# Rotary rounding one tile step later, and VectorE's query units behind the next maximum, in a hybrid decoder layer

## The reference, cut to what matters

```python
q = (_rmsnorm(c_q, q_norm_g) @ w_uq).reshape(b, s, MLA_HEADS, QK_NOPE + QK_ROPE)      # 8 heads, 64 + 32
kv = (_rmsnorm(c_kv, kv_norm_g) @ w_ukv).reshape(b, s, MLA_HEADS, QK_NOPE + V_HEAD)
q_rope = _apply_rope(q_rope, cos[:, :, None, :], sin[:, :, None, :])   # x1*cos - x2*sin, x2*cos + x1*sin
k_rope = _apply_rope(k_rope_raw, cos, sin)
...
sc = jnp.einsum('bqhd,bkhd->bhqk', qn, k_nope) + jnp.einsum('bqhr,bkr->bhqk', qr, k_rope)
sc = jnp.where(causal[None, None], sc.astype(jnp.float32) * scale, -jnp.inf)
p = jax.nn.softmax(sc, axis=-1).astype(v.dtype)
return jnp.einsum('bhqk,bkhd->bqhd', p, v)
```

## Time and profile before

| | |
|---|---|
| median of 3 runs | 2233.1 us (2231.65 to 2235.87) |
| the profiled execution | 2231.14 us, span 2229.3 us, mean granted TensorE clock 0.992 |
| PE busy over the span | 2145.4 us (96%) |
| DVE, ACT, POOL busy | 1367.7 us (61%), 979.3 us (44%), 405.3 us (18%) |
| attention's tile steps | about 1237 to 1441 us from the span's start |

### The profile page before, as it was taken

How to read it: one execution, slowest core, us unless ns; L and a number is a source line. 1 busy time by engine, 2 the same in 40 slices (tenths; PEclk the granted TensorE clock), 3 DMA queues, 4 the chain that set the end, 5 groups by cost and what they waited for, 6 DMA issues and landing times.

```text
span 2229.3 us, 25934 instructions
## 1 busy us (share of the span) xinstructions
PE 2145.4 (96%) x9837; PEld 1780.6 (80%) x9837; DVE 1367.7 (61%) x1719; ACT 979.3 (44%) x1559; POOL 405.3 (18%) x444
## 2 busy tenths in 40 slices
PE   5999999999999999999999888899899999999998
PEld 4888788878887888888888677788788888888886
DVE  7667865557587656211212788677856766557666
ACT  6443333334364776311323666545533333333444
POOL 3123320000032221000011455402213331000012
PEclk9999999999999999999999999999999999999999
DMA  3355442253442111222410100265335453216234
GB/s 123 95 171 186 159 166 71 68 196 102 153 161 84 52 52 50 76 67 66 134 43 25 29 10 10 104 218 194 108 103 190 165 193 119 71 51 228 94 137 156
DMA packets 220293, 249.85 MB, mean 112 GB/s; under 512 B 24261, under 2 KB 161546, under 8 KB 220170
## 3 DMA queue, kind: packets, MB, share of 16 engines
q1 hardware_dynamic: 220170, 248.19, 34.0%
HBM read 192.06 MB, written 55.57 MB: 111 GB/s over the span
## 4 chain that ended last, share of the span: by engine, by line
PE 86%; DVE 6%; ACT 3%; issue 2%; POOL 2%; DMA 0%; SPq 0%; POOLq 0%; ACTq 0%; DVEq 0%
PE ps L88 28%; PE ps L90 28%; PE ps L89 28%; PE ps L2322 1%; PE ps L2290 1%; ACT a_probs L2266 1%; POOL a_rot L2207 1%; DVE a_pt L98 1%; PE ps L361 0%; DVE a_s L2256 0%; DVE w_lo L98 0%; DVE entry_y L346 0%; DVE exit_x L1337 0%; DMA entry_x<-in_x_dram 0%; DVE ff_w_lo L98 0%
## 5 line engine op out<-in xcount | busy, mean ns | idle before, releaser
L98 DVE TENSOR_TENSOR ff_w_lo<-ff_raw,ff_w_hi 128x512 fp32r<-128x512 f32 x264 | 214.0, 814 | 171.8 <-ACT ff_w_hi L94 171.5
L88 PE MATMUL ps<-ff_t,ff_w_hi 128*128 128x512 f32 x704 | 274.1, 389 | 0.4 <-DVE ff_w_lo L98 0.2
L90 PE MATMUL ps<-ff_t,ff_w_lo 128*128 128x512 f32 x704 | 273.9, 389 | 0.0
L89 PE MATMUL ps<-ff_t,ff_w_hi 128*128 128x512 f32 x704 | 273.9, 389 | 0.0
L94 ACT ACTIVATE ff_w_hi<-ff_raw 128x512 fp32r<-128x512 f32 x264 | 164.9, 627 | 179.5 <-PE ps L90 173.0
L88 PE MATMUL ps<-d_b_hi,d_a_hi 128*128 128x512 f32 x608 | 237.5, 391 | 3.8 <-DVE d_a_lo L98 3.7
L90 PE MATMUL ps<-d_b_hi,d_a_lo 128*128 128x512 f32 x608 | 236.6, 389 | 0.0
L89 PE MATMUL ps<-d_b_lo,d_a_hi 128*128 128x512 f32 x608 | 236.6, 389 | 0.0
L98 DVE TENSOR_TENSOR w_lo<-w_raw,w_hi 128x1024 fp32r<-128x1024 f32 (+2 forms) x81 | 90.5, 1119 | 233.2 <-ACT w_hi L94 233.2
L88 PE MATMUL ps<-ff_b,ff_w_hi 128*128 128x512 f32 x528 | 208.0, 394 | 6.0 <-ACT ff_u2x L696 5.0
L89 PE MATMUL ps<-ff_b,ff_w_hi 128*128 128x512 f32 x528 | 206.8, 392 | 0.0
(11 more groups left out here) (301 smaller groups left out, 4297.6 us busy)
## 6 DMA issues: line engine op xcount, KB each, us to landing
ff_raw<-in_ffn_w_gate_dram SPq DMA_DIRECT2D x44, 512.0 KB, 3.9
ff_raw<-in_ffn_w_up_dram SPq DMA_DIRECT2D x44, 512.0 KB, 4.0
d_sums<-in_ffn_w_down_dram SPq DMA_DIRECT2D x44, 512.0 KB, 4.1
sums_scratch<-d_sums SPq DMA_DIRECT2D x88, 256.0 KB, 2.6
w_raw<-in_w_in_dram SPq DMA_DIRECT2D x32, 512.0 KB, 4.0
d_raw<-sums_scratch SPq DMA_DIRECT2D x24, 512.0 KB, 3.3
w_raw<-in_w_out_dram SPq DMA_DIRECT2D x24, 512.0 KB, 4.2
spill_scratch<-ff_st SPq DMA_DIRECT2D x44, 256.0 KB, 2.9
```

The source lines that it names most:

```text
L88: pe.matmul(out, lh, rh, start=start, stop=False, skip_group_check=go_on)
L89: pe.matmul(out, lh, rl, start=False, stop=False, skip_group_check=go_on)
L90: return pe.matmul(out, ll, rh, start=False, stop=stop, skip_group_check=go_on)
L98: return nc.vector.tensor_tensor(lo, src, as_f32(hi), ALU.subtract)
```

## The change: what it does

In `act_step` and `dve_step` the rope's rounding and low part are those of unit n - 2 and no longer n - 1. In `dve_step` a q unit is worked on one tile step later (step n + 1, behind the maximum of n + 1, the low parts of n - 1, rope's low part of another unit and `pair_lo`); a k unit stays in step n. In `pool_step` the normalisation of n comes ahead of the rope sum of n - 1. TensorE's order and ScalarE's unit rounding stay. No instruction is added or taken away.

```diff
         if n < HEADS * HEAD_TILES:
-            if n > 0 and self.beside(n - 1):
-                self.rope_act(act, self.beside(n - 1))
+            if n > 1 and self.beside(n - 2):
+                self.rope_act(act, self.beside(n - 2))
             self.exponent(act, n)
             if self.beside(n):
                 self.unit_act(act, self.beside(n))
@@ dve_step
         if n >= 2:
             self.turned_lo(dve, n - 2)
         if n < HEADS * HEAD_TILES:
-            if n > 0 and self.beside(n - 1):
-                self.rope_dve(dve, self.beside(n - 1))
+            if n > 1 and self.beside(n - 2):
+                self.rope_dve(dve, self.beside(n - 2))
             if s == 3 and h > 0 and h % 2 == 0:
                 self.pair_lo(dve, h // 2 - 1, slice(0, SEQ), h // 2)
             if n == HEADS * HEAD_TILES - 1:
                 self.pair_lo(dve, 3, half_of(0), 4)
-            if self.beside(n):
+            before = self.beside(n - 1) if n > 0 else None
+            if before and before[0] == "q":
+                self.unit_dve(dve, before)
+            if self.beside(n) and self.beside(n)[0] == "k":
                 self.unit_dve(dve, self.beside(n))
 
     def pool_step(self, pool, n):
+        self.normalise(pool, n)
         if n > 0 and self.beside(n - 1):
-            pool.wait_ge(self.S["norm_done"], 2 * n)
+            pool.wait_ge(self.S["norm_done"], 2 * n + 2)
             self.rope_pool(pool, self.beside(n - 1))
-        self.normalise(pool, n)
```

## The result

The changed kernel takes 2245.86 us (median of 4 runs, 2245.62 to 2248.57) against 2232.38 before: 13.5 us slower, ratio 1.0061 with an interval of 1.0044 to 1.0079. The forecast was 2239.9, slower, and its range ended at 2245.0. The profiled execution spans 2244.0 us, 14.7 more than before. All of it lies in the tile steps: from the first scores of head 0 to the last product it is 224.3 us (1232.35 to 1456.66) for 209.6 (1232.99 to 1442.55), 14.75 more. The changed kernel's trace comes to these first scores 0.64 us earlier, in work that the change doesn't touch, so that its last product starts only 14.1 us later.

A forecast was written before the change was run, and what follows sets the result against it. TensorE bounds the kernel (busy 176 of 204 us in the tile steps), VectorE nearly as full (162). Terms 5.2 + 2.0 - 0.4 = +6.8 us on the profiled 2231.1 give 2237.9, plus 2.0 to the median: 2239.9; 8-in-10 range 2232.5 to 2245.

The forecast's parts named there:

- Place 1: Hand-over from step 7 to the next head's step 1, 7 times: TensorE's wait moves from `turn` to the unit; +5.2 us.
- head 6: Hand-over from head 6 to 7, without a unit at step 1: low parts of tile 7 about 0.3 us later.
- Place 2: Step 3 of odd heads, 3 times: maximum of step 6 0.96 us late, 0.68 us carried into the hand-over; +2.0 us.
- rival (b): VectorE's lateness from step 3 is taken up before step 7, hand-overs cost nearer 0.5 each: +2.6 us, 2235.7; chance 0.25.
- Place 3: Step 1 of even heads, 4 times: earlier low parts against a later exponent and maximum, clock included; -0.4 us.
- The waits for exponents: TensorE's waits for exponents in the tile steps, 4.8 us before the change, would nearly go.
- The clock term of 0.7 us: Even heads of the kernel before: 0.7 us taken as lost to the lower clock behind the wait before `turn` of tile 2.
- Head 0: Scores of step 4 no longer wait 1.50 us for an exponent behind rope: 0.6 us gained.
- GpSimd's order: Rope sum behind the normalisation at the hand-over: costs nothing, since the sum already followed the normalisation of tile 7.
- rival (c): Longer TensorE pauses end at the lower clock; four more falls of 0.7 us add 2.8: 2242.7; chance 0.12.
- the upper end of (c): By the skill's rule each of nine new TensorE pauses is a candidate for a clock fall: 2246.

The follow-up runs named there:

- only7: The kernel before with the change made for the q units of step 7 alone: 2242.78 us, ratio 1.0044.
- ropes: The changed kernel with VectorE's q unit back in its own step, rope later and GpSimd's sum behind the normalisation: 2246.91 us, ratio 1.0065.
- ropes_pf: The kernel before with only rope's rounding and low part a step later, GpSimd's sum still ahead of the normalisation: 2234.68 us, ratio 1.0008.
- full_pf: The changed kernel with GpSimd's rope sum ahead of the normalisation again: 2255.88 us, ratio 1.0106.
- filled kernels: The changed kernel and the kernel before, each with unread transposes in nearly all TensorE pauses of the tile steps: 2240.91 and 2229.42 us.
- after_fill2: The changed kernel with unread transposes in nearly every TensorE pause of the tile steps: 2240.91 us, ratio 1.0040.
- only3: The kernel before with the change made for the q units of step 3 of odd heads alone: 2238.30 us, ratio 1.0027.

## Why the prediction was wrong, point by point

- **Place 1** was right, mechanism and size. At full clock the hand-over costs +0.60 to +0.63 us from even and about +0.94 from odd heads (only7), forecast 0.7 and 0.93; head 6 +0.26, forecast 0.3. The gain at `turn` (1.80 to 0.75) and its loss at the unit came as the sum had them.
- **Place 2** had the mechanism (VectorE idles for 1.93 us, the wait goes from tile 3 to tile 4), but the term was over-sized: 2.0 us forecast, OA +0.13 and about 0.10 us beyond place 1 in OB, 0.7 us for three heads. The maximum of step 6 does come late, 0.98 us by its distance from the product of step 3 (13.51 for 12.53, forecast 0.96), but OA is only 0.13 longer: most of it is taken up by step 7, which was rival (b).
- **Place 3** was under-sized: -0.4 us forecast. At full clock EA is +1.0 to +1.1 us in heads 2, 4 and 6, where my steps amount to 0.4 to 0.6 without the clock's share. The prediction has the path: rope's rounding and low part ahead of the maximum of step 4. What it didn't have is the weights' low part, lengthened by 0.74 us beside GpSimd's sum: ScalarE's `take` ends at 1295.35, but `add` starts at 1295.98, when that low part has ended, so `add`, `pair_hi` behind it and rope's rounding behind that are late by up to 0.6 us. By this timeline `turn` of tile 2 comes 0.30 us earlier than before and not 0.98, and some 0.5 of the 1.08 us are the lengthened low part, an estimate; no run took it out alone. The waits for exponents didn't go either (4.5 us), since a new one of 0.76 us stands in each even head. The clock term of 0.7 us for the kernel before was right: filling gives back 0.67 us each in heads 2 and 6. Head 0 gained 0.3 us ahead of its first product, forecast 0.6.
- **GpSimd's order** "costs nothing": wrong as a statement. It is worth 12 us with VectorE's unit early (ropes against ropes_pf) and the opposite, 10 us, with it late (full_pf). Within this change it was the better of the two, and the places where it helps or hurts were not in the sum.
- **The step that failed is the clock.** Without it, my terms for the order from head 0's first product to head 6's hand-over, 5.2 + 2.0 + 1.6 us, come to 8.8, and the filled kernels show 8.8 over the same heads. That this agrees is luck: place 1 measured 4.9, place 2 0.7 and place 3 3.1. For the clock, the sum took 1.4 us as given back in heads 2 and 6 and set down nothing for the changed kernel; four falls of 0.7 were rival (c). Over these heads the changed kernel is 7.6 us longer than its filled twin, the kernel before 1.3: net +6.3 where the sum has -1.4. With head 0's -0.3 us that gives 8.8 + 6.3 - 0.3 = 14.8, and the trace has 14.75 where the sum had 6.8.
- How large the clock's share is depends on the stretch. From the first scores to the last product filling takes 6.5 us from the changed kernel and 2.75 from the kernel before; with the 1.15 us put back that after_fill2 lost by its own filling, the clock's net share is 4.9 of 14.75 us. The medians of the runs give less, 5.0 and 2.8, or 3.3 net of 13.5 with the same 1.15. It is from a quarter to under a half of the loss, and the order is the rest.
- Rival (c) was the right one, at 0.12 and at under half its price: five stretches of the changed kernel, EA in three heads and EB behind two, are 0.9 to 2.1 us longer than in its filled twin, not 0.7. I had the price from one short fall; in head 2 of the changed kernel 12 us at 0.72 are 3.4 us of full clock, and the clock is low again at the next hand-over. The sentence of "TensorE: Matmul & The Clock Gate" in the Trainium skill (section "A second HAM failure mode: psum-queue depth-cycling"), that the clock swings where TensorE idles briefly and often enough between groups of matmuls, agrees with this trace: pauses of 1.17 and 0.76 us stand right before the fall, and each is shorter than the single one of 1.80 us that left the clock up. That their closeness is the cause wasn't tested. By that rule the prediction has 2246 for the upper end of (c), and 2245.9 was measured; that it meets so well is luck, since there weren't nine falls of 0.7 us.
- That prices don't add (21.9 us for the three places apart, 13.5 together) is at least in part the clock: only3's even stretches, unchanged in order, are longer by more than VectorE's lateness of 0.29 us. How much is the order of the queues wasn't separated, for the three kernels were not run filled.

## What to carry to other kernels

When an edit moves pauses of TensorE, price them twice: by their length, and by what the granted clock does behind them, which here was from a quarter to under a half of the loss. Filling the pauses with work nobody reads, in a kernel and its twin, separates the two and was itself worth 2.8 us; but check each filling against the pause at its place, since one with no pause to fill cost 1.15 us. When an instruction is put behind a wait, look at what the engine did in that wait before, for VectorE lost 1.9 us by standing where it had been working. Before moving an operation with both inputs in SBUF, lay GpSimd's timeline beside VectorE's.

## What the runs showed of the hardware that I had not expected

VectorE and GpSimd held each other up. VectorE's weights' low part (two inputs in SBUF) took 1.06 to 1.56 us when it started beside GpSimd's rope sum, 0.56 or 0.69 (by its width) otherwise; it ended 0.41 to 0.44 or 0.54 to 0.56 us behind the sum's end, as though it had begun some 0.14 us before that end. GpSimd's power on 128 numbers took 1.43 us beside `pair_lo` in the changed kernel and 0.92 in the kernel before, where it took 0.55 otherwise; in both it ended 0.41 us behind `pair_lo`. By the Trainium skill, "SBUF — State Buffer", section "Who interferes with whom", a VectorE instruction with two inputs in SBUF contends with a GpSimd instruction that reads SBUF, and by the same page's summary the second one to issue is blocked altogether until the first has finished; both cases agree, but for these 0.14 us. A low part whose first input is in PSUM showed no such lengthening: in head 3 of the changed kernel one of 128x512 began at 1332.46 under the rope sum of 1331.45 to 1332.71 and took 0.67 us.

The clock isn't repeatable from a pause's length alone: the same pause of 1.48 us before `turn` of tile 2 was followed by the lower level in head 2 of the kernel before and not in head 4.
